# Stick-breaking attention: running sums from a rounded part and a rest, the two heads of a pair side by side

## The chip, the cores and the metric

One core of one Trainium2 chip. The metric is the device time of one execution in microseconds (us); lower is better.

## What is computed

The program is two layers of a hybrid block (feed-forward, a mixer of three branches, feed-forward) on 256 tokens of width 1024, and then a third block of another kind (delta rule, window attention, experts). The change is in one branch of the mixer, stick-breaking attention with 16 heads of 64:

```python
def _stick_breaking(qc, kc, vc):
    ...
    def block(args):
        qblk, qp = args
        z = jnp.einsum('bqhd,bkhd->bhqk', qblk, k).astype(jnp.float32) * scale
        strict = kpos[None, :] < qp[:, None]
        log_stay = jnp.where(strict, jax.nn.log_sigmoid(-z), 0.0)
        after = lax.cumsum(log_stay, axis=3, reverse=True) - log_stay
        a = jnp.where(strict, jnp.exp(jax.nn.log_sigmoid(z) + after), 0.0)
        return jnp.einsum('bhqk,bkhd->bqhd', a.astype(v.dtype), v)
```

The running sum over the keys is what the change is about. The kernel holds scores with the keys on the partitions, so that a running sum over keys is a product with a triangular matrix of ones.

## The kernel before

Most of the time goes to dense products whose weights stream in. A chunk of weights (128x1024 f32) is loaded by SyncE, ScalarE rounds it to fp32r (`hi`, L252), VectorE makes the rest (`lo`, L256), and TensorE adds three products, hi by hi, lo by hi and hi by lo (`three`, L281 to L283). The ring holds six chunks, so that rounding and splitting run up to six chunks ahead of the products.

Each engine has one queue, written out by hand. In the mixer (`Mixer.pe`, `.act`, `.dve`, L1719 on) the order follows a counter `h`, half a chunk of dense work on TensorE, and small steps of the branches are hung on values of `h`. Stick-breaking works on eight pairs of heads, one every five steps of `h` (`STICK = 5`; `pair_at(h, at)` gives the pair whose step `at` falls on `h`). A pair j has these steps, with the `h` of pair 0:

- TensorE, h = 5: `scores` (L1275, L1276), f32, into two banks, one for each head. The banks are shared by pairs of one parity.
- VectorE, h = 6: `dve_logits` scales and masks both heads (L1324) and takes the absolute value as max(-z, z) (L1327).
- ScalarE, h = 7: `act_log`, Exp (L1306) and Ln (L1308).
- VectorE, h = 9: `dve_stay` adds the positive part (L1332).
- TensorE, h = 10: `sums`, which waits for `stay`. For each head it is an f32 product with the triangle `from_` over 384 columns (L1284) and one with `ones` over 128 (L1285).
- VectorE, h = 11: `dve_shift` subtracts the sums from the logits (L1337).
- ScalarE, h = 12: `act_weights`, Exp (L1313).
- TensorE, h = 13: `outputs` (L1298 to L1300), f32.
- ScalarE, h = 14: `act_out` copies the 128x256 outputs out of PSUM (L1317). `scores` of pair j + 2 waits for it.

So `scores` of a pair and `sums` of the pair before it stand next to each other on TensorE. Near the end of the eight pairs the third branch starts: ScalarE makes a convolution's first tap at h = 42, 44 and 46 (L1361), VectorE the others from h = 44 to 52 (L1369, 4 instructions at each h), ScalarE applies Silu at h = 48, 51 and 54 (L1379). TensorE makes decays at h = 50 (L1461 to L1464), VectorE turns them into a table at h = 51 (`dve_cum`, its last instruction L1558), and TensorE turns the convolution's result at h = 54 (`turn_x`, L1470), which waits for that table.

GpSimd has a queue of its own. In the mixer it loads parameters, clears a pad and computes a power for another branch (L1105), and then waits for far later work. Elsewhere it multiplies rows for the third block (L910, L912) and splits a few chunks (L270).

## Time and profile before

| what | before |
|---|---|
| median of 3 runs | 2263.89 us (2263.28 to 2265.24) |
| the profiled execution, first to last instruction | 2268.0 us |
| that execution's own time, as far as recorded | its span, nothing around it is given |
| busy, TensorE matmul | 2207.9 us (97% of the span) |
| busy, VectorE | 1621.7 us (72%) |
| busy, ScalarE | 1161.0 us (51%) |
| busy, GpSimd | 364.9 us (16%) |
| mean granted TensorE clock | 0.980 |

The span is longer than the median of the runs without a profile by 4.1 us (0.2%). Busy shares are of one engine; a busy TensorE is one with a matmul in flight, and its instructions overlap by their pipelining, so that what a product costs is read from the distance of two starts. The steps of stick-breaking lie from about 372 to 472 us in the first layer and from about 1190 to 1290 us in the second.

### The profile page before, as it was taken

The numbers are of one execution on the slowest core, as the hardware profiler recorded it, in microseconds if no ns is written. First come the engines' busy times: TensorE is split into PE (matmuls) and PEld (weight loads), VectorE is DVE, ScalarE is ACT, GpSimd is POOL, SyncE is SP. The second block draws the span as 40 slices with busy tenths as digits, with TensorE's granted clock in tenths as the row PEclk, the third lists the DMA queues.
The fourth block names the chain that finished last, engine by engine and source line by source line (L and its number), as shares of the span: only waits on it lengthen the run. The fifth ranks groups of instructions, "written<-read, shape, count | busy, mean of one in ns | idle before, by whom it ended". The sixth has DMA issues, their size and how long they took to land.

```text
span 2268.0 us, 33371 instructions
## 1 busy us (share of the span) xinstructions
PE 2207.9 (97%) x12388; PEld 1862.2 (82%) x12388; DVE 1621.7 (72%) x2101; ACT 1161.0 (51%) x1720; POOL 364.9 (16%) x177
## 2 busy tenths in 40 slices
PE   7999999999999999999999999999988998999999
PEld 6888898878888888888988788788887987887777
DVE  5776676688767767766766798677687635658997
ACT  4445465575454444445555654444455515447875
POOL 1541000000025513511000000144202300000000
PEclk9999999999999999999999999999989877999999
DMA  9765644344667658756543345587542005559996
GB/s 307 232 229 165 206 146 135 118 149 140 203 213 238 227 170 262 231 185 204 158 141 122 120 158 186 169 262 237 185 145 76 3 6 164 188 189 320 360 360 220
DMA packets 320169, 426.92 MB, mean 188 GB/s; under 512 B 28192, under 2 KB 220080, under 8 KB 320032
## 3 DMA queue, kind: packets, MB, share of 16 engines
q1 hardware_dynamic: 315904, 412.45, 56.0%
q0 software_dynamic: 4016, 12.63, 2.1%
q8 instruction: 84, 1.38, 0.2%
q14 instruction: 53, 0.43, 0.1%
q10 hardware_dynamic: 112, 0.04, 0.0%
HBM read 423.97 MB, written 1.05 MB: 187 GB/s over the span
## 4 chain that ended last, share of the span: by engine, by line
PE 89%; DVE 6%; issue 1%; ACT 1%; DMA 1%; DVEq 1%; POOL 1%; SPq 0%; POOLq 0%; ACTq 0%
PE ps L281 20%; PE ps L283 20%; PE ps L282 20%; PE ps L644 10%; PE ps L3670 4%; DVE lo L256 1%; DVE room L1369 1%; PE ps L1284 1%; PE ps L630 1%; PE ps L331 1%; POOL lo L270 1%; PE ps L1126 1%; PE ps L2597 1%; PE ps L2581 1%; PE ps L2591 0%
## 5 line engine op out<-in xcount | busy, mean ns | idle before, releaser
L256 DVE TENSOR_TENSOR lo<-raw,hi 128x1024 fp32r<-128x1024 f32 (+1 forms) x727 | 1003.2, 1399 | 361.9 <-ACT hi L252 353.8
L252 ACT CAST hi<-raw 128x1024 fp32r<-128x1024 f32 (+1 forms) x737 | 766.2, 1048 | 581.2 <-PE ps L283 437.8
L281 PE MATMUL ps<-hi,xT_hi 128*128 128x512 f32 x1392 | 555.0, 399 | 5.9 <-issue 4.4
L283 PE MATMUL ps<-hi,xT_lo 128*128 128x512 f32 x1392 | 543.3, 390 | 0.0
L282 PE MATMUL ps<-lo,xT_hi 128*128 128x512 f32 x1392 | 542.5, 390 | 0.0
L281 PEld LDWEIGHTS ps<-hi,xT_hi 128*128 128x128 f32 x1392 | 262.8, 189 | 58.1 <-issue 6.0
L283 PEld LDWEIGHTS ps<-hi,xT_lo 128*128 128x128 f32 x1392 | 262.5, 189 | 56.0
L282 PEld LDWEIGHTS ps<-lo,xT_hi 128*128 128x128 f32 x1392 | 263.0, 189 | 50.4
L910 POOL TENSOR_SCALAR room<-room,vecs 128x1536 f32<-128x1536 f32 x28 | 133.3, 4762 | 233.7 <-DMA room<-in_w_ada 233.7
L281 PE MATMUL ps<-xT_hi,hi 128*128 128x256 f32 (+1 forms) x560 | 164.7, 294 | 0.9 <-DVE xT_lo L2350 0.9
L283 PE MATMUL ps<-xT_hi,lo 128*128 128x256 f32 (+1 forms) x560 | 159.4, 285 | 0.0
L282 PE MATMUL ps<-xT_lo,hi 128*128 128x256 f32 (+1 forms) x560 | 159.4, 285 | 0.0
L644 PE MATMUL ps<-hi,hidT_hi 128*128 128x512 f32 x352 | 137.6, 391 | 0.0
L644 PE MATMUL ps<-hi,hidT_lo 128*128 128x512 f32 x352 | 137.3, 390 | 0.0
L644 PE MATMUL ps<-lo,hidT_hi 128*128 128x512 f32 x352 | 137.0, 389 | 0.0
L281 PEld LDWEIGHTS ps<-xT_hi,hi 128*128 128x128 f32 (+1 forms) x560 | 106.9, 191 | 5.7 <-issue 5.0
L282 PEld LDWEIGHTS ps<-xT_lo,hi 128*128 128x128 f32 (+1 forms) x560 | 106.9, 191 | 0.4
L283 PEld LDWEIGHTS ps<-xT_hi,lo 128*128 128x128 f32 (+1 forms) x560 | 106.7, 190 | 0.3
L912 POOL TENSOR_TENSOR room<-room 128x1536 f32<-128x1536 f32 x28 | 103.0, 3679 | 8.1 <-issue 4.7
L281 PE MATMUL ps<-hi,brT_hi 128*128 128x512 f32 x224 | 90.5, 404 | 1.7 <-DVE brT_lo L341 1.7
L283 PE MATMUL ps<-hi,brT_lo 128*128 128x512 f32 x224 | 89.1, 398 | 0.0
L282 PE MATMUL ps<-lo,brT_hi 128*128 128x512 f32 x224 | 89.0, 397 | 0.0
(546 smaller groups left out, 3156.6 us busy)
## 6 DMA issues: line engine op xcount, KB each, us to landing
raw<-in_w_mix_in SPq DMA_DIRECT2D x368, 256.0 KB, 2.9
raw<-in_ffn_w_in SPq DMA_DIRECT2D x352, 256.0 KB, 3.3
raw<-in_ffn_w_out SPq DMA_DIRECT2D x176, 256.0 KB, 2.9
raw<-in_w_gate SPq DMA_DIRECT2D x128, 256.0 KB, 4.9
raw<-in_w_up SPq DMA_DIRECT2D x128, 256.0 KB, 6.6
raw<-in_w_down SPq DMA_DIRECT2D x128, 256.0 KB, 5.5
room<-in_w_ada SPq DMA_DIRECT2D x32, 768.0 KB, 6.4
raw<-in_w_branch SPq DMA_DIRECT2D x96, 256.0 KB, 2.9
```

The lines of the kernel that those rows point to most:

```text
L252: nc.scalar.copy(hi[c.hi_slot][:, 0:c.cols], raw[c.slot][:, 0:c.cols]).then_inc(rounded, 1)
L256: nc.vector.tensor_tensor(lo[c.slot][:, 0:c.cols], raw[c.slot][:, 0:c.cols], hi[c.hi_slot][:, 0:c.cols], ALU.subtract).then_inc(split, 1)
L270: nc.gpsimd.tensor_tensor(lo[c.slot][:, 0:c.cols], raw[c.slot][:, 0:c.cols], hi[c.hi_slot][:, 0:c.cols], ALU.subtract).then_inc(split, 1)
L281: pe.matmul(out, a[0], b[0], start=start, stop=False)
L282: pe.matmul(out, a[0], b[1], start=False, stop=False)
L283: return pe.matmul(out, a[1], b[0], start=False, stop=stop)
L331: ins = pe.transpose(ps[:, bank, at:at + P], self.src[:, t, k * P:(k + 1) * P], ident)
L630: ins = pe.transpose(ps[:, 6 + t, k * P:(k + 1) * P], hid[:, t, k * P:(k + 1) * P], ident)
L644: ins = pe.matmul(ps[:, 2 * t + half, :], a[p], w[q][:, cols], start=first and n == 0, stop=False, skip_group_check=True)
L910: nc.gpsimd.tensor_scalar(self.rows(k), self.rows(k), cols2[:, k:k + 1], None, ALU.mult)
L912: nc.gpsimd.tensor_tensor(pieces.acc, pieces.acc, self.rows(k), ALU.add).then_inc(pieces.multiplied, 1)
L3670: ins = pe.matmul(ps[:, self.sums(tile) + half, :], a[p], w[q][:, cols], start=first and n == 0, stop=False, skip_group_check=True)
```

## The change

The logarithms' sums (`stay`) are rounded to fp32r by ScalarE (`act_round`), the rest is made by GpSimd (`pool_rest`), and the sums are six fp32r products for a pair in place of four f32 ones. For that the two heads of a pair lie side by side, in three blocks of 2x128 columns: one block of 256 columns is the last key block, the other 512 fill a bank. `dve_logits` reorders them and takes two instructions for it. The outputs are copied by VectorE (`dve_out`) and no longer by ScalarE. The steps are moved: `sums` from h = 10 to 12, `dve_shift` from 11 to 13, `act_weights` from 12 to 14, `outputs` from 13 to 15, the copy of the outputs from 14 to 16; `act_round` is at h = 10. `scores` of pair j + 2 now waits for `shifted` of pair j, and `sums` for the copy of pair j - 2. Semaphores of two other classes are merged (`Scan`, `DeltaRule`) with the same waits as before; that part of the diff is left out but for one line.

```diff
         ("ident", p == j),
         ("ones", np.ones((P, P))),
+        ("from_", p >= j),
         ("upto", p <= j),
-        ("from_", p >= j),
...
-        z, lg = ([view(t, at + 768 * j, 2, 384) for t, at in ((scratch, 0), (room, R_GATES))] for j in range(2))
+        z = [view(scratch, 768 * j, 3, 2, P) for j in range(2)]
+        lg = [view(room, R_GATES + 768 * j, 3, 2, P) for j in range(2)]
+        lg_hi = [over(f"stick_hi{j}", [P, 768], "merged", 768 * j) for j in range(2)]
+        lg_lo = [over(f"stick_lo{j}", [P, 768], "room", R_GATES + 768 * j) for j in range(2)]
+        sum_ones = over("stick_ones", [P, 2 * P], "room", R_GATES + 1536)
...
         def scores(self, pe, j):
             g = j % 2
             if j > 1:
-                pe.wait_ge(self.copied, self.nth(j - 2))
+                pe.wait_ge(self.shifted, self.nth(j - 2))
...
         def sums(self, pe, j):
             g = j % 2
-            pe.wait_ge(self.stay, self.nth(j))
-            for e in range(2):
-                bank = ps[:, 2 * g + e, :]
-                pe.matmul(bank[:, 0:384], const("from_"), self.lg[g][:, e, :], start=True, stop=False)
-                ins = pe.matmul(bank[:, P:TOK], const("ones"), self.lg[g][:, e, TOK:384], start=False, stop=True)
-            ins.then_inc(self.summed, 1)
+            pe.wait_ge(self.rest, self.nth(j))
+            if j > 1:
+                pe.wait_ge(self.copied, self.nth(j - 2))
+            ones, from_ = self.sum_ones[:, 0:P], self.sum_ones[:, P:2 * P]
+            hi_, lo_ = self.lg_hi[g], self.lg_lo[g]
+            first, last = ps[:, 2 * g, :], ps[:, 2 * g + 1, 0:TOK]
+            pe.matmul(first, from_, hi_[:, 0:512], start=True, stop=False)
+            pe.matmul(first, from_, lo_[:, 0:512], start=False, stop=False)
+            pe.matmul(last, from_, hi_[:, 512:768], start=True, stop=False)
+            pe.matmul(last, from_, lo_[:, 512:768], start=False, stop=True)
+            pe.matmul(first[:, TOK:512], ones, hi_[:, 512:768], start=False, stop=False)
+            pe.matmul(first[:, TOK:512], ones, lo_[:, 512:768], start=False, stop=True).then_inc(self.summed, 1)
...
+        def act_ones(self, act):
+            act.wait_ge(consts_par, 16)
+            at = CONSTS["ones"][0]
+            nc.scalar.copy(self.sum_ones[:], consts[:, at:at + 2 * P])
+
+        def act_round(self, act, j):
+            g = j % 2
+            act.wait_ge(self.stay, self.nth(j))
+            nc.scalar.copy(self.lg_hi[g][:], self.lg[g].rearrange("p n e k -> p (n e k)")).then_inc(self.rounded, 1)
+
+        def pool_rest(self, eng, j):
+            g = j % 2
+            eng.wait_ge(self.rounded, self.nth(j))
+            nc.gpsimd.tensor_tensor(self.lg_lo[g][:], self.lg[g].rearrange("p n e k -> p (n e k)"), self.lg_hi[g][:], ALU.subtract).then_inc(self.rest, 1)
...
-        def act_out(self, act, j):
-            act.wait_ge(self.out_done, self.nth(j))
-            nc.scalar.copy(br[:, :, j * P:(j + 1) * P], self.out(j % 2)).then_inc(self.copied, 1)
+        def dve_out(self, dve, j):
+            dve.wait_ge(self.out_done, self.nth(j))
+            if j + 2 < self.PAIRS:
+                dve.wait_ge(self.scored, self.nth(j + 2))
+            nc.vector.tensor_copy(br[:, :, j * P:(j + 1) * P], self.out(j % 2)).then_inc(self.copied, 1)
 
         def dve_logits(self, dve, j):
...
-            V.scalar_tensor_tensor(out=self.z[g], in0=ps[:, 2 * g:2 * g + 2, 0:384], scalar=HDC ** -0.5,
-                                   in1=bc(const("stick_add").unsqueeze(1), [P, 2, 384]), op0=ALU.mult, op1=ALU.add)
+            mask = const("stick_add").rearrange("p (n k) -> p n k", n=3)
+            for e in range(2):
+                V.scalar_tensor_tensor(out=self.z[g][:, :, e, :], in0=ps[:, 2 * g + e, 0:384].rearrange("p (n k) -> p n k", n=3), scalar=HDC ** -0.5,
+                                       in1=mask, op0=ALU.mult, op1=ALU.add)
...
-        dt_abs, dt_log, decay_done = sem("b_dt_abs"), sem("b_dt_log"), sem("b_decay")
...
     # Mixer.pe
-                j = self.pair_at(h, 10)
+                j = self.pair_at(h, 12)
                 if j is not None:
                     stick.sums(pe, j)
-                j = self.pair_at(h, 13)
+                j = self.pair_at(h, 15)
                 if j is not None:
                     stick.outputs(pe, j)
...
     # Mixer.act
-                j = self.pair_at(h, 12)
+                if h == 8:
+                    stick.act_ones(act)
+                j = self.pair_at(h, 14)
                 if j is not None:
                     stick.act_weights(act, j)
                 j = self.pair_at(h, 7)
                 if j is not None:
                     stick.act_log(act, j)
-                j = self.pair_at(h, 14)
+                j = self.pair_at(h, 10)
                 if j is not None:
-                    if j == 0:
-                        act.wait_ge(feat_turned, self.turn_a.value(3))
-                    stick.act_out(act, j)
+                    stick.act_round(act, j)
...
     # Mixer.dve
-                j = self.pair_at(h, 11)
+                j = self.pair_at(h, 13)
                 if j is not None:
                     stick.dve_shift(dve, j)
+                j = self.pair_at(h, 16)
+                if j is not None:
+                    if j == 0:
+                        dve.wait_ge(feat_turned, self.turn_a.value(3))
+                    stick.dve_out(dve, j)
...
     # Layer.pool
             m.scan.load_norm(pool)
+            for j in range(StickBreaking.PAIRS):
+                m.stick.pool_rest(pool, j)
             pool.wait_ge(evac_dve, m.A.gate[1].evac_dve)
```

The lines of the changed kernel are other ones than those before: `scores` is L1279 and L1280 there, `sums` L1291 to L1296, `outputs` L1308 to L1310, the logarithm L1316 and L1318, the rounding L1328, the rest L1333, the weights' Exp L1338, the copy of outputs L1344, the logits L1353 and L1356, `stay` L1361, `shift` L1367, the taps L1391 and L1399, Silu L1409.

How the sums stand on TensorE. This is the difference on TensorE at h = 12 of the first layer, between two half chunks of dense work (L281 to L283):

```order
 L282 MATMUL ps<-xT_lo,hi_61 128x256
 L283 MATMUL ps<-xT_hi,lo_49 128x256
+L1291 MATMUL ps<-stick_hi_96,stick_ones 128x512 [waits c_rest]
+L1292 MATMUL ps<-stick_lo_98,stick_ones 128x512
+L1293 MATMUL ps<-stick_hi_96,stick_ones 128x256
+L1294 MATMUL ps<-stick_lo_98,stick_ones 128x256
+L1295 MATMUL ps<-stick_hi_96,stick_ones 128x256
+L1296 MATMUL ps<-stick_lo_98,stick_ones 128x256
 L281 MATMUL ps<-xT_hi,hi_61 128x256
 L282 MATMUL ps<-xT_lo,hi_61 128x256
```

The sums now stand alone between fp32r products; the outputs of pair j - 2 have moved to where they were, behind the scores of pair j.

The end of the eight pairs on VectorE, from h = 43 on, before:

```order
L256 TENSOR_TENSOR lo_57<-raw,hi_63 128x1024
L1332 SCALAR_TENSOR_TENSOR room<-room 128x768
L1369 SCALAR_TENSOR_TENSOR room<-room,vecs 128x256 x8
L256 TENSOR_TENSOR lo_58<-raw,hi_64 128x1024
L1337 TENSOR_TENSOR room<-room,ps 128x768
L1369 SCALAR_TENSOR_TENSOR room<-room,vecs 128x256 x8
```

and of the change, from the same chunk on:

```order
L256 TENSOR_TENSOR lo_57<-raw,hi_63 128x1024
L1361 SCALAR_TENSOR_TENSOR room<-ln_par,room 128x768
L1399 SCALAR_TENSOR_TENSOR room<-room,vecs 128x256 x8
L256 TENSOR_TENSOR lo_58<-raw,hi_64 128x1024
L1344 COPY hidden<-ps 128x2x128
L1399 SCALAR_TENSOR_TENSOR room<-room,vecs 128x256 x8
L256 TENSOR_TENSOR lo_59<-raw,hi_65 128x1024
L1367 TENSOR_TENSOR ln_par<-ln_par,ps 128x768
L1399 SCALAR_TENSOR_TENSOR room<-room,vecs 128x256 x8
```

The shift of pair 7 (L1337 before, L1367 now) has moved behind eight more taps, one more chunk and a copy of outputs.

The same end on ScalarE in the change, from h = 45 on:

```order
L1328 CAST stick_hi_97<-room 128x768
L252 CAST hi_64<-raw 128x1024
L1391 ACTIVATE room<-room,vecs 128x256 x4
L252 CAST hi_65<-raw 128x1024
L1409 ACT_TABLE_LOAD
L1409 ACTIVATE room<-room 128x1024
L1338 ACT_TABLE_LOAD
L1338 ACTIVATE ln_par<-ln_par 128x768
L1563 ACT_TABLE_LOAD
```

The weights of pair 7 (L1338) now come behind the first Silu, with a load of tables before them and one after.

## Rows read from the trace of the kernel before

**Rows 1.** The page, busy time of each engine.

```profile
PE 2207.9 (97%) x12388; PEld 1862.2 (82%) x12388; DVE 1621.7 (72%) x2101; ACT 1161.0 (51%) x1720; POOL 364.9 (16%) x177
```

**Rows 2.** Waits of TensorE, whole span: us in total, times, longest.

```profile
PE ps L1284 <- DVE room L1332: 4.1, 2, 2.1
PE ps L1284 <- DVE ln_par L1332: 2.9, 2, 1.4
...
PE ps L1470 <- DVE small L1558: 1.4, 2, 1.2
```

**Rows 3.** The chain of waits that ended last, 440 to 490 us: start, us, what.

```profile
450.88 0.64 PE ps L1275 x4
...
456.60 0.85 ACT room L1306
...
460.80 0.96 ACT hi L252
461.78 1.23 DVE lo L256
...
482.39 1.09 PE ps L1470 x8
```

**Rows 4.** Timeline of TensorE, scores and sums at h = 15: start, us.

```profile
394.69 0.28 PE L282 MATMUL ps<-xT_lo,hi 128*128 128x256 f32 x1
394.81 0.28 PE L283 MATMUL ps<-xT_hi,lo 128*128 128x256 f32 x1
395.02 0.71 PE L1275 MATMUL ps<-room 64*128 64x256 f32 x4
...
395.88 0.91 PE L1284 MATMUL ps<-room,consts 128*128 128x384 f32 x2
...
397.64 0.36 PE L281 MATMUL ps<-xT_hi,hi 128*128 128x256 f32 x1
397.84 0.28 PE L282 MATMUL ps<-xT_lo,hi 128*128 128x256 f32 x1
```

**Rows 5.** Timeline of TensorE, two neighbouring fp32r products of 512 columns.

```profile
480.15 0.39 PE L282 MATMUL ps<-lo,xT_hi 128*128 128x512 f32 x1
480.38 0.39 PE L283 MATMUL ps<-hi,xT_lo 128*128 128x512 f32 x1
```

**Rows 6.** Timeline of TensorE, outputs of pair 6 and what follows.

```profile
457.61 0.33 PE L1298 MATMUL ps<-room,ln_par 128*128 128x64 f32 x2
...
458.86 0.48 PE L281 MATMUL ps<-hi,xT_hi 128*128 128x512 f32 x1
```

**Rows 7.** Source L270: split of a chunk by GpSimd, ns min/median/max.

```profile
L270 POOL TENSOR_TENSOR lo<-raw,hi x10: 2397/2410/2417, 204.8 to 1464.4; 128x1024 fp32r<-128x1024 f32 x10
```

**Rows 8.** Groups of VectorE by form: busy us, mean ns of one.

```profile
L1235 DVE SCALAR_TENSOR_TENSOR ln_par<-room,ln_par 128x256 f32<-128x256 f32 x16 | 7.7, 479 | 0.0
L1324 DVE SCALAR_TENSOR_TENSOR room<-ps,consts 128x768 f32<-128x768 f32 x8 | 7.6, 950 | 0.0
L1211 DVE COPY room<-ps 128x256 f32<-128x256 f32 x16 | 6.7, 420 | 2.4 <-PE ps L1114 2.4
```

**Rows 9.** Timeline of VectorE and GpSimd, 59 to 67 us.

```profile
59.77 6.50 DVE L256 TENSOR_TENSOR lo<-raw,hi 128x1024 fp32r<-128x1024 f32 x3
...
59.41 3.51 POOL L912 TENSOR_TENSOR room<-room 128x1536 f32<-128x1536 f32 x1 [0.42 <-issue]
```

**Rows 10.** Timeline of VectorE, shift of pair 7 and the taps behind it.

```profile
468.61 0.95 DVE L1337 TENSOR_TENSOR room<-room,ps 128x768 f32<-128x768 f32 x1
469.48 3.25 DVE L1369 SCALAR_TENSOR_TENSOR room<-room,vecs 128x256 f32<-128x256 f32 x8
```

**Rows 11.** Timeline of ScalarE, a load of tables before the first Silu.

```profile
471.40 1.28 ACT L1379 ACT_TABLE_LOAD   x1
```

**Rows 12.** Windows, first layer, from sums 0 to sums 7: PE, PEld, DVE, ACT busy.

```profile
384.27:461.88 77.61, 77.50 (x501) 65.92 (x499) 48.11 (x57) 41.27 (x60) 0.00 (x0) 1.00 0.37 117
```

**Rows 13.** Windows, first layer, behind the wait of sums 7: granted clock is 0.50.

```profile
466.00:468.00 2.00, 2.00 (x7) 1.65 (x6) 1.93 (x5) 0.90 (x2) 0.00 (x0) 0.50 0.00 0
```

82 lines of the change are left out of this document (45 added, 37 removed).

## The prediction

> **What bounds the kernel now.** I read the busy shares first: TensorE has a matmul in flight for 97% of the span, VectorE works 72%, ScalarE 51%, GpSimd 16% [rows 1]. So a step costs what it takes on TensorE's queue, unless TensorE waits. Next the waits of TensorE: it waits for the logarithms (L1332) in front of the sums four times, 7.0 us in all, 1.4 us at pair 0 and 2.1 us at pair 7 in each layer, and twice for the decay table (L1558), 1.4 us in all [rows 2]. Then the chain of waits at the end of the eight pairs. It leaves TensorE behind the scores of pair 7 (start 450.88), goes over VectorE and ScalarE (Exp at 456.60, rounding of a chunk at 460.80), and from 461.78 on lies in VectorE's queue until TensorE's turn of the convolution at 482.39 [rows 3]. The reader should see two regimes in each layer: up to the scores of pair 7 the time is TensorE's, and from there to h = 54 it is VectorE's queue. What TensorE saves in the second stretch is worth nothing by itself.
>
> **TensorE, up to the scores of pair 7.** The f32 sums of a pair run from 395.88 to 397.64, 1.76 us [rows 4]. The new ones are two fp32r products of 512 columns and four of 256. Neighbours of these sizes start 0.23 us [rows 5] and 0.12 us [rows 4] apart, so 2 x 0.23 + 4 x 0.12 = 0.94 us, a saving of 0.82 us for a pair. Six pairs' sums (0 to 5) lie before this point: 4.9 us.
>
> Each group of f32 products also costs its borders. The scores start 0.21 us behind a product whose successor is due after 0.12, and behind the sums the second fp32r product comes 0.20 us after the first instead of 0.12 [rows 4]: 0.17 us for a group. Before, scores with the sums of the pair ahead were one group and outputs another, 14 up to here. Now the scores carry the outputs of pair j - 2 and the sums are fp32r, so that there are 8. Six fewer give 1.0 us. The outputs of pair 5, 1.25 us [rows 6], move behind this point; I count them below.
>
> The waits here: sums 0 waited 1.4 us. They now come two half chunks later. A half chunk is 12 products of 256 or 6 of 512 columns, 1.4 us either way, so 2.8 us, and a turn of eight transposes between them adds about 1. After the logarithms come a rounding, 3/4 of a chunk's 0.96 us [rows 3], and the rest on GpSimd, 3/4 of the 2.41 us of a chunk's split [rows 7], 1.8 us. GpSimd starts behind VectorE's next chunk, 1.2 us after the logarithms. The rest is there 1.4 + 1.2 + 1.8 + 0.1 = 4.5 us after TensorE's old arrival and TensorE 3.8 us after it: a wait of 0.7, a gain of 0.7.
>
> The middle pairs: from scores to sums TensorE now has seven half chunks (9.8), two groups of outputs (2.3), one of scores (0.9) and one of sums (0.9), 13.9 us. The chain behind the scores is: outputs of pair j - 2 (1.1), their copy (0.4), logits, the logarithm (two of 0.85 [rows 3]), a rounding of a chunk (1.0), its split (1.2), the shift of pair j - 1 (0.9), for even pairs the weights' Exp and another chunk on ScalarE (1.9; stay and the rounding lie beside it), that chunk's split, behind which GpSimd stands (1.2), and the rest (1.8). The logits in two instructions: 256 columns take 479 ns and 768 take 950 [rows 8], so 384 take about 0.60 and two 1.2, 0.25 us more than now. The copy is bounded by one of the same shape, 420 ns [rows 8]. With 2.2 for the logits, 1.7 for the logarithm and 0.4 for hand-overs the sum for an even pair is 13.8 us, a tie with 13.9; odd pairs have 2 us to spare. I charge 0.4 us for each of pairs 2, 4 and 6, 1.2 us; the bounds are 0 and a whole rest each, 5.4 us.
>
> Up to the scores of pair 7 a layer gains 4.9 + 1.0 + 1.25 + 0.7 - 1.2 = 6.65 us.
>
> **From there to h = 54.** The scores end 0.86 us [rows 4] after their start, at S = 451.7, and the turn starts at S + 30.7 [rows 3]. Before, the logits of pair 7 ended with the Exp's start at 456.6, S + 4.9, because the sums of pair 6 and their shift stood ahead of them. Now outputs 5, a copy, two halves and the absolute value do: 1.1 + 0.4 + 1.2 + 1.0 = 3.7. From there to VectorE's chunk at 461.78 it is 5.2 us of ScalarE as before, so S + 8.9 where it was S + 10.1. From that chunk to the turn it is 20.6 us [rows 3] of VectorE's queue. What joins it: the copies of pairs 6 and 7 (0.4 each) and what the rest of pair 7 on GpSimd takes from VectorE. No row shows GpSimd under the taps (L1369). The nearest is three chunks' splits from 59.77 on that take 6.50 us where three of 1.2 would take 3.6: they lose 2.9 us under a GpSimd product that ends at 62.92, 3.15 us after they began [rows 9]. So the cost lies between 0 and the 1.8 us of a rest; I take 1.8, as the taps too read two operands from SBUF. The Trainium skill, SBUF — State Buffer, section on the two separate sides, says that a VectorE instruction with two SBUF inputs and a GpSimd instruction that reads SBUF lock each other out for a whole instruction. By that rule the taps are held for the full rest and the term is as taken; if only some instructions were held, it would be smaller and the sum better by up to 3.6 us over the layers.
>
> S + 8.9 + 20.6 + 0.8 + 1.8 = S + 32.1, 1.4 us later than now. TensorE comes out at the same place. Its sums 7 wait some 1.5 us for the rest. The shift of pair 7 was 6.8 us behind that chunk's start (468.61 [rows 10]); eight more taps (3.25 [rows 10]), a chunk (1.2), a copy and the GpSimd's 1.8 stand ahead of it now, so it ends at S + 8.9 + 6.8 + 6.7 + 0.9, S + 23.3. With the Exp the outputs of pair 7 start at S + 24.2, where TensorE is ready at about S + 19.8: a new wait of over 4 us. Outputs, decays and four half chunks (7.8) end at S + 32.0. What stands behind that wait is all dense work, but VectorE's queue would hold it anyway.
>
> **What costs nothing.** Two more loads of tables in a layer, 1.28 us each [rows 11], fall on ScalarE while it would wait for the shift or has room before the next Silu, which itself waits for VectorE's taps; if that cover were gone, they cost 2.6 us a layer. The copy of the ones, once a layer, is under 0.4 us on ScalarE. The scores' new wait (for the shift of pair j - 2) ends earlier than their place. GpSimd has nothing behind the rests but parameter loads that waited until after h = 55. SyncE's queue is not touched. The reordered constants and merged semaphores move nothing.
>
> **The sum.** A layer gains 6.65 - 1.4 = 5.25 us, two layers 10.5. The profiled execution, 2268.0 us, would become 2257.5. The runs' median of 2263.89 is 4.1 us below it; the same difference there gives 2253.4 us. Behind h = 54 the queues stand to each other as before, so the gain stays.
>
> **Rivals.** (A) The waits go for good and VectorE's queue is not lengthened: the rest of pair 7 finds room, the even pairs' tie falls well. Then a layer gains eight savings (6.6), the borders (1.0) and the waits of 1.4 and 2.1 (3.5): 11.1, so 2241.7 us. For it speaks that VectorE is busy 48.1 of 77.6 us between sums 0 and 7 [rows 12]; against it the solid stretch from 461.78 on. Chance 0.13.
>
> (B) The move does nothing for the time. The even pairs wait 1.3 us each, and the long wait before outputs 7 costs clock too: after the wait of 2.1 us at sums 7 TensorE was granted 0.50, the lower level of 1.2 GHz, between 466 and 468 us [rows 13], which costs some 1.6 us. A layer gains 5.25 - 2.7 - 1.6 = 1, so 2262 us. Chance 0.15.
>
> (C) Slower. The rest is late for every pair, because GpSimd and VectorE hold each other: each rest takes its 1.8 us, the wait for a VectorE chunk ahead (1.2) and a start-up, and VectorE in turn loses 1.8 us to it, which moves the next logits. The chain of a pair then grows by 3 us; even pairs wait 3.4 and odd pairs 1. From 0.8 us of wait for every pair on, the gain is gone. With 2.2 on average, a layer loses 8 x 2.2 against the 6.65 + 1.2 gained before waits and the 1.4 behind S: 11 us a layer, 2286 us; with 1.6 it is 2277. Against it speaks that VectorE's chunks are rounded and split up to six ahead, so that it has slack between the steps. Chance 0.04.
>
> (D) The change doesn't do what it says, the fp32r products being no faster than f32 ones: 2268 with the later steps. Rows 4 and 5 exclude nearly all of it; it is in the 0.04.
>
> **How the numbers follow.** The forecast has 0.68, A 0.13, B 0.15, C with D 0.04. The forecast's own range takes in the bounds of its terms, 3.6 us better without the hold, and 5 worse with 0.9 us more wait for each even pair: 2249 to 2259. For 8 in 10 I go half way into A and to B: 2246 to 2261. A measurement can tell 0.2%, 4.5 us, so faster means below 2259.4: nearly all of the forecast, all of A and little of B, 0.83; the same 0.13; slower 0.04.
>
> **What would show it.** The sums (L1291 to L1296) should take 0.94 us a pair, and the windows up to the scores of pair 7 should be 6 to 7 us shorter in each layer. TensorE's list of waits should hold L1291 for the rest (L1333), under 1 us for even pairs and 1.5 us at pair 7, and one of about 4 us at the outputs of pair 7 (L1308). The rest should take 1.8 us, and taps beside it should show one stretched instruction. The turn of the convolution should come 32 us after the scores of pair 7. The prediction is wrong if waits at L1291 sum to over 10 us, if VectorE's queue from its chunk to the table takes no longer than 20.6 us, or if what is gained by h = 54 is lost behind it.

## The result and the profile after

The changed kernel is slower: 2275.74 us median (2271.85 to 2279.14, 6 runs) against 2264.56 us (2263.28 to 2267.59, 6 runs) before, ratio 1.004, interval 1.003 to 1.005: 0.4%, small but clear of noise. The forecast was 2253.4 us. In a second comparison (e12_change_again) it is 2274.38 against 2265.33, ratio 1.0039, 1.0025 to 1.0052. The profiled execution took 2276.91 us and its span is 2275.1 us, with a mean granted clock of 0.973 where it was 0.980.

The page of the changed kernel, busy time of each engine, answers to [rows 1]:

```profile
PE 2204.6 (97%) x12356; PEld 1863.0 (82%) x12356; DVE 1648.3 (72%) x2133; ACT 1172.2 (52%) x1726; POOL 397.3 (17%) x193
```

TensorE is hardly less busy, although 16 pairs' sums are 0.82 us shorter each. Either they are not shorter, or something else was lengthened. The timeline of TensorE, changed kernel, sums of pair 2 (start, us), answers to [rows 4]:

```profile
397.79 0.40 PE L1291 MATMUL ps<-stick_hi,stick_ones 128*128 128x512 f32 x1
398.02 0.40 PE L1292 MATMUL ps<-stick_lo,stick_ones 128*128 128x512 f32 x1
398.26 0.28 PE L1293 MATMUL ps<-stick_hi,stick_ones 128*128 128x256 f32 x1
398.38 0.28 PE L1294 MATMUL ps<-stick_lo,stick_ones 128*128 128x256 f32 x1
398.50 0.28 PE L1295 MATMUL ps<-stick_hi,stick_ones 128*128 128x256 f32 x1
398.61 0.28 PE L1296 MATMUL ps<-stick_lo,stick_ones 128*128 128x256 f32 x1
398.73 0.28 PE L281 MATMUL ps<-xT_hi,hi 128*128 128x256 f32 x1
```

From 397.79 to 398.73 it is 0.94 us, as worked out. The waits of TensorE over the whole span (us in total, times, longest) answer to [rows 2]:

```profile
PE ps L1308 <- ACT ln_par L1338: 7.7, 4, 4.0
PE ps L1279 <- DVE ln_par L1367: 5.9, 2, 2.9
...
PE ps L1291 <- POOL stick_lo L1333: 0.8, 2, 0.4
```

The waits in front of the sums are nearly gone (7.0 us before, 0.8 now). In their place stand two that the change made: the outputs (L1308) wait for the weights' Exp, and the scores of pair 7 (L1279) wait 2.9 us in each layer for a shift. The windows of the first layer around these two show the clock (the number after POOL's busy time):

```profile
444.00:448.00 4.00, 1.19 (x6) 0.65 (x4) 2.03 (x3) 1.87 (x3) 0.00 (x0) 1.00 0.44 131
448.00:452.00 4.00, 3.88 (x21) 3.63 (x22) 2.15 (x3) 3.46 (x4) 1.31 (x1) 0.58 0.02 6
452.00:456.00 4.00, 4.00 (x12) 3.14 (x12) 3.86 (x6) 1.45 (x2) 0.81 (x1) 0.56 0.05 4
...
472.00:476.00 4.00, 1.38 (x12) 1.38 (x13) 3.93 (x8) 2.58 (x4) 0.00 (x0) 1.00 0.06 22
476.00:480.00 4.00, 4.00 (x16) 3.04 (x16) 2.26 (x5) 4.00 (x4) 0.00 (x0) 0.50 0.00 0
480.00:484.00 4.00, 4.00 (x14) 3.11 (x13) 3.77 (x11) 2.88 (x4) 0.00 (x0) 0.65 0.43 131
```

Behind each wait TensorE is granted 0.50, its lower level of 1.2 GHz, for some 7 us, and does half as much. Added up over windows of 1 us, one such stretch cost 3.4 us of full clock (5.1, in 10 us, behind the outputs of pair 7 in the second layer). TensorE counts as fully busy in it, which is why its busy time did not fall.

The table puts the two layers side by side: starts of scores 0, of scores 7 and of the turn at h = 54; TensorE's waits in front of stick-breaking's steps and the turn; and the clock lost, which is the sum of one minus the granted clock over windows of 1 us.

| | scores 0 | scores 7 | turn | scores 0 to turn | waits | clock lost |
|---|---|---|---|---|---|---|
| before, layer 0 | 371.92 | 450.81 | 482.39 | 110.47 | 3.7 | 1.7 |
| before, layer 1 | 1190.39 | 1269.29 | 1300.88 | 110.49 | 5.1 | 0 |
| changed, layer 0 | 372.06 | 448.12 | 485.55 | 113.49 | 7.6 | 6.8 |
| changed, layer 1 | 1193.80 | 1269.86 | 1308.01 | 114.21 | 6.8 | 8.5 |

The change loses 3.0 and 3.7 us between scores 0 and the turn, nearly all of what the span grew (7.1 us); behind the turn both kernels take the same time (967.1 us from the second turn to the end, in both). The medians lie 11 us apart, 4 more than the two spans: the span before was 3.4 us above the median of its runs, the span after 0.6 us below its own.

### The profile page after: what moved, and what is told of

Its sections match the earlier page's. It is cut to its first block, busy times and chain, and to the rows that moved or that the text cites. A ratio compares the mean times of both kernels' runs of the same rounds, so it can differ in the third digit from the quotient of the medians.

```text
span 2275.1 us, 33383 instructions
## 1 busy us (share of the span) xinstructions
PE 2204.6 (97%) x12356; PEld 1863.0 (82%) x12356; DVE 1648.3 (72%) x2133; ACT 1172.2 (52%) x1726; POOL 397.3 (17%) x193
## 4 chain that ended last, share of the span: by engine, by line
PE 85%; DVE 7%; ACT 2%; issue 2%; DVEq 1%; DMA 1%; POOL 1%; SPq 0%; POOLq 0%; ACTq 0%
PE ps L281 20%; PE ps L283 19%; PE ps L282 19%; PE ps L644 10%; PE ps L3715 4%; DVE lo L256 2%; DVE room L1399 1%; ACT hi L252 1%; PE ps L630 1%; PE ps L331 1%; PE ps L1126 1%; DVE room L1356 1%; DVEq L1355 1%; PE ps L2642 1%; PE ps L2626 0%
## 5 line engine op out<-in xcount | busy, mean ns | idle before, releaser
L256 DVE TENSOR_TENSOR lo<-raw,hi 128x1024 fp32r<-128x1024 f32 (+1 forms) x727 | 1015.3, 1416 | 362.1 <-ACT hi L252 354.3
L281 PE MATMUL ps<-hi,xT_hi 128*128 128x512 f32 x1392 | 557.8, 401 | 5.9 <-issue 4.4
L283 PE MATMUL ps<-hi,xT_lo 128*128 128x512 f32 x1392 | 546.7, 393 | 0.0
L281 PEld LDWEIGHTS ps<-hi,xT_hi 128*128 128x128 f32 x1392 | 265.2, 190 | 59.0 <-issue 6.0
L283 PEld LDWEIGHTS ps<-hi,xT_lo 128*128 128x128 f32 x1392 | 264.5, 190 | 56.8
L281 PE MATMUL ps<-xT_hi,hi 128*128 128x256 f32 (+1 forms) x560 | 163.9, 293 | 0.9 <-DVE xT_lo L2394 0.9
L283 PE MATMUL ps<-xT_hi,lo 128*128 128x256 f32 (+1 forms) x560 | 158.7, 283 | 0.0
L281 PEld LDWEIGHTS ps<-xT_hi,hi 128*128 128x128 f32 (+1 forms) x560 | 106.1, 190 | 5.9 <-issue 5.0
L283 PEld LDWEIGHTS ps<-xT_hi,lo 128*128 128x128 f32 (+1 forms) x560 | 106.1, 189 | 0.3
L281 PE MATMUL ps<-hi,brT_hi 128*128 128x512 f32 x224 | 90.9, 406 | 1.7 <-DVE brT_lo L341 1.7
L283 PE MATMUL ps<-hi,brT_lo 128*128 128x512 f32 x224 | 89.6, 400 | 0.0
```

The lines of the kernel that those rows point to most:

```text
L256: nc.vector.tensor_tensor(lo[c.slot][:, 0:c.cols], raw[c.slot][:, 0:c.cols], hi[c.hi_slot][:, 0:c.cols], ALU.subtract).then_inc(split, 1)
L281: pe.matmul(out, a[0], b[0], start=start, stop=False)
L283: return pe.matmul(out, a[1], b[0], start=False, stop=stop)
```

## The experiments

Two theories of the wait at the scores of pair 7. **L**: it is a loop through the queues. The scores of pair j need the shift of pair j - 2. The chain of waits of the changed kernel, 439 to 449 us (start, us, what), shows it going from the logits of pair 6 over ScalarE into the chunk's split, behind which the shift of pair 5 stands:

```profile
441.25 0.93 DVE ln_par L1353 x2
442.18 0.07 issue
442.26 0.97 DVE room L1356
...
443.25 0.84 ACT room L1316
...
444.92 1.03 ACT hi L252
445.95 0.02 issue
445.97 1.22 DVE lo L256
447.20 0.88 DVE ln_par L1367
448.07 0.04 issue
448.12 0.73 PE ps L1279 x4
```

The shift needs none of this; the last product of its sums started at 440.81. It stands at h = 13 behind the split of the chunk, the chunk's cast stands on ScalarE behind the logarithm of the next pair, and that needs the next pair's logits, which stand on VectorE behind the steps of the pair before. So a pair cannot take less than this round through the two queues, and the logits of pairs 4 to 7 start 11.7 us apart on average (417.36 to 452.41) where TensorE would take 10.2 to 10.8. The two engines fall behind from pair to pair: the logits of pairs 4, 5 and 6 start 3.9, 5.3 and 6.7 us behind their scores, and at pair 7 TensorE has to wait.

**G**: GpSimd's rests hold VectorE. The timelines of VectorE and GpSimd, changed kernel, around two rests:

```profile
427.41 1.67 DVE L1576 TENSOR_TENSOR small<-room,vecs 128x32 f32<-128x32 f32 x1
...
437.21 0.19 DVE L1585 SCALAR_TENSOR_TENSOR small<-small,vecs 128x32 f32<-128x32 f32 x1
...
438.89 2.03 DVE L256 TENSOR_TENSOR lo<-raw,hi 128x1024 fp32r<-128x1024 f32 x1 [0.88 <-ACT hi L252]
...
426.88 2.16 POOL L1333 TENSOR_TENSOR stick_lo<-room,stick_hi 128x768 fp32r<-128x768 f32 x1 [10.86 <-ACT stick_hi L1328]
437.98 1.86 POOL L1333 TENSOR_TENSOR stick_lo<-room,stick_hi 128x768 fp32r<-128x768 f32 x1 [8.95 <-ACT stick_hi L1328]
```

An operation on 32 columns takes 1.67 us and ends with the rest (429.08, the rest at 429.04); its like outside a rest takes 0.19. A split takes 2.03 us instead of 1.23, and ends 1.08 us after the rest's end (439.84). The Trainium skill, SBUF — State Buffer, section on the two separate sides, says that the two engines lock each other out for a whole instruction when VectorE reads two operands from SBUF and GpSimd's instruction reads SBUF too; these rows agree.

In the tables below each experiment's ratio is to the kernel before in the same comparison, with its 95% interval.

### The two theories, one relief each

e1_no_rest: the rests are left out, and the products of the rest read the rounded part a second time, so the part of the logarithms that rounding loses is missing in the sums.

```diff
-            pe.wait_ge(self.rest, self.nth(j))
+            pe.wait_ge(self.rounded, self.nth(j))
...
-            hi_, lo_ = self.lg_hi[g], self.lg_lo[g]
+            hi_, lo_ = self.lg_hi[g], self.lg_hi[g]
...
-            for j in range(StickBreaking.PAIRS):
-                m.stick.pool_rest(pool, j)
```

> The changed kernel without GpSimd's rests: the products with the rest read the rounded part a second time and wait for the rounding, so TensorE does the same six products and the sums are less exact. Theory L (loop): VectorE and ScalarE pass each other work in a loop of about 11.6 us a pair against 10.4 us on TensorE, because a weight chunk's rounding stands behind the rounding of the logarithms on ScalarE and the shift stands behind that chunk's split on VectorE; GpSimd is only a small part: 2270 to 2274 us, the wait of TensorE at the scores of pair 7 still over 1 us. Theory G (GpSimd holds VectorE): each rest stretches one VectorE instruction by 0.6 to 1.5 us and that is what fills the loop: the wait at the scores is gone, the one at the outputs of pair 7 is under 2.5 us, 2256 to 2264 us.

e2_shift12: `dve_shift` at `pair_at(h, 12)` instead of 13, which puts it ahead of the split.

```diff
-                j = self.pair_at(h, 13)
+                j = self.pair_at(h, 12)
                 if j is not None:
                     stick.dve_shift(dve, j)
```

> The changed kernel with VectorE's shift one step earlier (h = 12 in place of 13), which puts it ahead of a weight chunk's split for every other pair. Theory L: the wait of 2.9 us at the scores of pair 7 goes in both layers, and with it the lower clock behind it (some 3 us a layer); the wait at the outputs of pair 7 gets shorter, as the shift then stands ahead of four taps and a chunk: 2262 to 2268 us. Theory G: the shift's place doesn't matter, as the queue is as full as before: 2273 to 2277 us.

e3_cast_first: `act_round` behind the chunk's cast at the end of the step.

```diff
-                j = self.pair_at(h, 10)
-                if j is not None:
-                    stick.act_round(act, j)
...
                 if h % 2 and h > 1:
                     tick_act(act, b.chunks[c])
+                j = self.pair_at(h, 10)
+                if j is not None:
+                    stick.act_round(act, j)
```

> The changed kernel with ScalarE's rounding of the logarithms behind the weight chunk's rounding of the same step, not ahead of it (odd pairs alone have both in one step). Theory L: the chunk no longer waits for stay, each odd pair takes about 1.5 us less in the loop, the wait at the scores of pair 7 goes: 2264 to 2270 us. Theory G: 2273 to 2277 us, since the rests hold VectorE as before.

e4_copy_act: the copies of the outputs on ScalarE again, still at h = 16. The logits of pair j + 2 now wait for the copy, as another engine makes it.

```diff
-                dve.wait_ge(self.out_done, self.nth(j - 2))
+                dve.wait_ge(self.copied, self.nth(j - 2))
...
+                    stick.act_out(act, j)
...
-                    stick.dve_out(dve, j)
```

> The changed kernel with the copy of the outputs on ScalarE again (at h = 16, the logits of pair j + 2 wait for it). It takes 0.4 us a pair off VectorE's queue and puts 0.4 us and a hand-over on ScalarE's. Theory L: a loop that goes over both engines gains nothing, as the logits now wait for ScalarE: 2273 to 2280 us. Theory G (VectorE is simply too full): 0.4 us a pair less on VectorE shortens the waits by 1 to 3 us a layer: 2269 to 2273 us.

| | median us | ratio | wait at scores 7 | scores 0 to turn, layers 0 and 1 |
|---|---|---|---|---|
| e1_no_rest | 2260.62 | 0.9979 (0.9970 to 0.9988) | none | 107.1, 107.1 |
| e2_shift12 | 2260.37 | 0.9981 (0.9971 to 0.9992) | none | 106.9, 107.1 |
| e3_cast_first | 2265.98 | 0.9999 (0.9990 to 1.0008) | 0.38 | 110.2, 108.8 |
| e4_copy_act | 2270.36 | 1.0017 (1.0008 to 1.0026) | 2.30 | 112.1, 109.5 |

Each theory was right about its own relief and wrong about the other's: L had named 2270 to 2274 us for e1_no_rest, G 2273 to 2277 for e2_shift12. So in this kernel each cause is needed for the wait and neither is enough. The round is set by the order, and it is too long by what the rests add to it; to relieve it at either place is enough. Moving one operation by a half chunk, with every rest in place, gives 2260.4 us, better than L had said (2262 to 2268, the half clock behind the wait included). The wait at the outputs of pair 7 fell with it, from 3.96 and 3.25 us to 2.6, and the clock lost behind it in the second layer from 5.1 to 3.4. In e1_no_rest that wait was 3.3 us, where G had named under 2.5. Of stick-breaking's steps in the second layer of e2_shift12, behind pair 0, these alone still waited (timeline of TensorE; the wait stands in brackets):

```profile
1268.10 0.43 PE L1308 MATMUL ps<-room,ln_par 128*128 128x64 f32 x2 [0.62 <-ACT ln_par L1338]
...
1272.96 0.50 PE L1291 MATMUL ps<-stick_hi,stick_ones 128*128 128x512 f32 x1 [0.49 <-POOL stick_lo L1333]
...
1280.89 0.43 PE L1308 MATMUL ps<-room,ln_par 128*128 128x64 f32 x2 [2.63 <-ACT ln_par L1338]
```

e3_cast_first is in L's range (2264 to 2270), though 0.38 us of the wait stayed. e4_copy_act moved 0.4 us a pair off VectorE and left most of the wait: the copy is a small part of the loop. It is in G's range (2269 to 2273) and below L's (2273 to 2280).

### The products alone, both reliefs, and the Exp

e5_f32_sums undoes the arithmetic and keeps the order; `act_ones`, `act_round` and `pool_rest` are left out with it.

```diff
-            pe.wait_ge(self.rest, self.nth(j))
+            pe.wait_ge(self.stay, self.nth(j))
...
+            lg = self.lg[g].rearrange("p n e k -> p (n e k)")
...
-            pe.matmul(first, from_, hi_[:, 0:512], start=True, stop=False)
-            pe.matmul(first, from_, lo_[:, 0:512], start=False, stop=False)
-            pe.matmul(last, from_, hi_[:, 512:768], start=True, stop=False)
-            pe.matmul(last, from_, lo_[:, 512:768], start=False, stop=True)
-            pe.matmul(first[:, TOK:512], ones, hi_[:, 512:768], start=False, stop=False)
-            pe.matmul(first[:, TOK:512], ones, lo_[:, 512:768], start=False, stop=True).then_inc(self.summed, 1)
+            pe.matmul(first, from_, lg[:, 0:512], start=True, stop=False)
+            pe.matmul(last, from_, lg[:, 512:768], start=True, stop=True)
+            pe.matmul(first[:, TOK:512], ones, lg[:, 512:768], start=False, stop=True).then_inc(self.summed, 1)
```

> The changed kernel with the sums in f32 again (three products instead of six, read from the logarithms themselves): no rounding, no rest, no copy of the ones; the layout, the later places of all steps and VectorE's copies stay. TensorE gets 0.82 us a pair more (6.6 a layer), VectorE is rid of GpSimd's hold and ScalarE of the rounding (0.83 us a pair). Theory G (GpSimd's hold makes the loop late): no wait at L1279, few waits before the sums, 2258 to 2266 us, below the changed kernel's 2275.7 although TensorE has more to do. Theory L (it is the place of the shift behind h = 13 in VectorE's queue that closes the loop): the wait at the scores of pair 7 stays at 1 us or more and the time is 2268 to 2276. If the moved steps alone were the whole loss, it would be above 2280.

e6_shift_cast is e2_shift12 with e3_cast_first.

> The changed kernel with both reliefs of the loop: the shift at h = 12 and the rounding behind the chunk's cast on ScalarE. Each alone took the wait at the scores of pair 7 away. Theory L: the second has little left to relieve, 2258 to 2262, as with the shift alone (2260.4). If what is left of the loss is the late logarithm of pair 7 and not the loop, the later rounding makes the wait at the sums longer (1.4 us or more at pair 7) and it is 2261 to 2266.

e7_shift_weights is e2_shift12 with `act_weights` at `pair_at(h, 13)` instead of 14.

> The changed kernel with the shift at h = 12 and the weights' Exp at h = 13, so that the Exp of pair 7 stands ahead of the first Silu (h = 48) in ScalarE's queue and no table is loaded back and forth there. Theory K (the wait of 2.6 us at the outputs of pair 7 costs itself and then half the clock for about 3 us in each layer): the wait falls under 1.2 us, no half clock behind it, 2254 to 2258. Theory V (VectorE's queue holds the turn of the convolution anyway): the wait shrinks, a wait appears at the turn or the decays instead, 2259 to 2262.

e8_rest_vector is e7_shift_weights with the rest on VectorE at h = 11.

```diff
-            nc.gpsimd.tensor_tensor(self.lg_lo[g][:], ...
+            nc.vector.tensor_tensor(self.lg_lo[g][:], ...
...
+                j = self.pair_at(h, 11)
+                if j is not None:
+                    stick.pool_rest(dve, j)
```

> As e7_shift_weights, but the rest of the logarithms is made by VectorE at h = 11 (about 1 us a pair) and not by GpSimd. Theory G (under a rest of GpSimd VectorE loses about as much as the rest would take it itself, some 7 us a layer): within 3 us of e7_shift_weights, no VectorE instruction stretched in the eight pairs. If the hold were cheap (under 0.3 us a pair), VectorE would be 5 to 6 us a layer more busy and the time 4 us or more above e7_shift_weights.

| | median us | ratio | scores 0 to scores 7 | scores 0 to turn |
|---|---|---|---|---|
| e5_f32_sums | 2267.53 | 1.0011 (1.0002 to 1.0020) | 75.8 | 110.3, 109.0 |
| e6_shift_cast | 2260.30 | 0.9979 (0.9970 to 0.9988) | 72.4 | 107.2, 107.1 |
| e7_shift_weights | 2265.88 | 1.0001 (0.9992 to 1.0010) | 73.1 | 108.8, 108.5 |
| e8_rest_vector | 2264.76 | 1.0003 (0.9994 to 1.0013) | 74.0 | 109.3, 108.4 |

With f32 sums in the same order there is no wait at the scores of pair 7, and the kernel is faster than the changed one by 8 us with more work on TensorE. So the new places alone do not lose what the change lost (2.5 us of the 11 stay). That the wait went fits the rests and the rounding being gone from the round, but TensorE is also slower here (its scores 4 to 7 start 11.0 to 11.4 us apart), which leaves the round more time; this run does not part the two. It came out 1.5 us above the range that G named and 0.5 below L's, whose wait of 1 us or more is absent; a wait of 2.6 us at the outputs of pair 7 and 3.4 and 1.7 us of clock lost behind it are there too.

e6_shift_cast shows that the second relief adds nothing to the first. The wait at the sums of pair 7 grew to 1.42 us, and the one at its outputs shrank from 2.64 to 1.85. e7_shift_weights was a miss for both of its theories. To save two loads of tables the Exp of every pair was moved a half chunk ahead, into a place where ScalarE stands and waits for the shift with the casts behind it: the wait at the sums of pair 7 grew from 0.48 to 1.74 us, and the turn waited for VectorE by 2.7 us in layer 1.

e8_rest_vector weighs the hold. The windows of the first layer from 372.9 to 452.7 us (TensorE, weight load, VectorE, ScalarE, GpSimd), e7_shift_weights:

```profile
372.90:452.70 79.80, 77.73 (x532) 68.46 (x531) 64.22 (x90) 45.30 (x61) 13.85 (x8) 1.00 0.42 131
```

and e8_rest_vector:

```profile
372.90:452.70 79.80, 77.30 (x531) 68.47 (x530) 64.32 (x96) 45.18 (x61) 0.60 (x1) 1.00 0.41 129
```

Its rests among VectorE's groups (busy us, mean ns of one):

```profile
L1333 DVE TENSOR_TENSOR stick_lo<-room,stick_hi 128x768 fp32r<-128x768 f32 x16 | 15.2, 952 | 0.0
```

VectorE is busy 64.2 us with the rests on GpSimd, and 64.3 with the rests its own, each 0.95 us. The two windows do not hold quite the same instructions. e10_pair7_cum and e14_no_rest_pair7, which come below, differ in the rests alone and do, 129 in each from scores 0 to the turn:

```profile
371.97:473.91 101.94, 99.14 (x649) 86.33 (x648) 85.48 (x129) 63.67 (x85) 15.81 (x9) 1.00 0.43 132
371.20:471.18 99.98, 98.79 (x650) 86.33 (x649) 79.32 (x129) 63.69 (x85) 0.60 (x1) 1.00 0.42 133
```

So eight rests on GpSimd stretch VectorE's instructions by 6.2 us, 0.77 us each. Making a rest on GpSimd took four fifths or more of the VectorE time that making it there takes. The time of e8_rest_vector, 1.1 us below e7_shift_weights, is within the 3 us that G had named; with it came a wait of 4.4 us at the sums of pair 7, for VectorE's rest.

### The tail of pair 7, and the clock

In e2_shift12 the outputs of pair 7 still waited 2.6 us, and 7 us at half clock followed. Three versions ask what that wait is worth.

e9_pair7_early:

```diff
-                j = self.pair_at(h, 13)
+                j = 7 if h == 46 else self.pair_at(h, 12) if h != 47 else None
                 if j is not None:
                     stick.dve_shift(dve, j)
...
-                j = self.pair_at(h, 14)
+                j = 7 if h == 47 else self.pair_at(h, 14) if h != 49 else None
                 if j is not None:
                     stick.act_weights(act, j)
```

> The changed kernel with the shift at h = 12 for pairs 0 to 6 and, for pair 7 alone, the shift at h = 46 on VectorE (ahead of a copy and two groups of taps) and the weights' Exp at h = 47 on ScalarE (ahead of the first Silu). With the shift at h = 12 alone the shift of pair 7 stood at 462.37 us though its sums were complete at 459.0, and its Exp started at 464.86 behind the first Silu and a table load. Theory K (a wait of 2.6 us at the outputs of pair 7 costs itself and half the clock for 7 us behind it): the outputs of pair 7 wait under 0.5 us, the granted clock stays at 1.00 up to the turn, and a layer gains 3 us or more: 2252 to 2256 us. Theory V (VectorE's queue, busy but for 0.4 us from the stay of pair 7 to the turn, holds the turn anyway): the wait comes back at the turn or the decays, a layer gains 0 to 1.3 us: 2258 to 2261.

e10_pair7_cum adds to it:

```diff
-                if h == 51:
+                if h == 50:
                     scan.dve_cum(dve, 1)
```

> As e9_pair7_early, and the copies of the decay sums (the four small operations that the turn waits for) at h = 50 on VectorE, ahead of a chunk's split, an addition and a copy. Theory V: the turn no longer waits for VectorE's queue, 2 us a layer below e9_pair7_early if that had a wait at the turn, 2254 to 2257. Theory K: no difference from e9_pair7_early (within 1.5 us), since there was no wait at the turn.

e11_outputs_later is e2_shift12 with:

```diff
-                j = self.pair_at(h, 15)
+                j = 7 if h == 52 else self.pair_at(h, 15) if h != 50 else None
                 if j is not None:
                     stick.outputs(pe, j)
...
-                j = self.pair_at(h, 16)
+                j = 7 if h == 53 else self.pair_at(h, 16) if h != 51 else None
```

> The changed kernel with the shift at h = 12, and the outputs of pair 7 at h = 52 instead of h = 50 on TensorE (their copy at h = 53): two more half chunks (2.7 us) ahead of them, the length of the wait that they had (2.64 us). Nothing is taken from VectorE or ScalarE. Theory K (the wait and the half clock behind it): no wait of over 0.5 us, clock 1.00 up to the turn; TensorE is 4 us a layer earlier at the turn unless VectorE holds it: 2252 to 2257 us. Theory V: the turn waits instead, 2259 to 2262. If the half clock is set by something other than the idle time of TensorE, it appears here too.

e12_change_again is the changed kernel itself.

> The changed kernel as it is, once more, beside the three others on the same chip. All theories: 2272 to 2279 us, ratio to before 1.003 to 1.005, with waits of 2.9 us at the scores of pair 7 and 3.2 to 4.0 at its outputs in both layers, each followed by the granted clock 0.50 for 6 to 8 us.

| | median us | ratio | outputs 7 wait | turn waits | clock lost up to the turn | scores 0 to turn |
|---|---|---|---|---|---|---|
| e9_pair7_early | 2260.76 | 0.9980 (0.9971 to 0.9989) | none | 4.1 | 0 | 105.3, 105.3 |
| e10_pair7_cum | 2257.12 | 0.9964 (0.9951 to 0.9978) | none | 0.7 | 0 | 101.9, 101.9 |
| e11_outputs_later | 2262.98 | 0.9990 (0.9981 to 0.9999) | none | 4.2 | 0, 0.4 | 105.4, 105.4 |
| e12_change_again | 2274.38 | 1.0039 (1.0025 to 1.0052) | 4.0 | none | 6.8, 6.8 | 113.8, 114.0 |

Each of the two theories was half right. The wait at the outputs went, and the clock stayed at 1.00 up to the turn (K); but the time came back as a wait at the turn, for the copies of the decay sums in VectorE's queue, and e9_pair7_early is no faster than e2_shift12 (V). Waits of TensorE, e9_pair7_early:

```profile
PE ps L1507 <- DVE small L1595: 8.1, 2, 4.1
...
PE ps L1291 <- POOL stick_lo L1333: 1.8, 4, 0.5
```

In e11_outputs_later the half clock appeared at the wait at the turn instead (3.4 us lost in each layer, in layer 1 from within the wait on), so that it follows TensorE's idle time wherever that is; it was slower than either theory had said. e10_pair7_cum fell 0.1 us above what V named (2254 to 2257), 3.6 us below e9_pair7_early and so 2.1 below what K allowed. In its trace four small operations (L1591 to L1595) no longer stand behind four taps, two additions for a gate (L1055) and a copy, and it has the clock at 1.00 throughout (windows of e10_pair7_cum, first layer):

```profile
468.00:476.00 8.00, 7.26 (x36) 5.81 (x35) 7.69 (x19) 5.97 (x5) 0.00 (x0) 1.00 0.44 133
476.00:484.00 8.00, 5.85 (x29) 4.35 (x28) 6.73 (x13) 5.58 (x6) 0.00 (x0) 1.00 0.43 130
```

e10_pair7_cum beats both kernels: 0.36% below the one before, 17 us below the changed one. Not all of the turn's gain is kept: from the second turn to the end of the span it takes 970.2 us where the two kernels take 967.1, since behind the turn VectorE and ScalarE come last (a second turn waits 0.9 us in each layer for VectorE's copy; the overlaps, L1515, wait 1.3 us in each layer for ScalarE's copies).

### What the products are worth in the right order

e13_f32_pair7 is e10_pair7_cum with the edit of e5_f32_sums; e14_no_rest_pair7 is e10_pair7_cum with that of e1_no_rest, so the same part of the sums is missing.

> As e10_pair7_cum (the places of the steps as there), but with the sums in f32 again, no rounding, no rest, no copy of the ones: what the rounded products are worth once the order is right. Theory T (TensorE's time up to the scores of pair 7 counts in full, as 0.82 us a pair): 6.5 us a layer above e10_pair7_cum's 2257.1, less what TensorE waited there, 2266 to 2271. Theory H (GpSimd's hold on VectorE and the rounding give back most of it, VectorE's queue ends the stretch): 2257 to 2263.

> As e10_pair7_cum, without GpSimd's rests: the second product of each pair reads the rounded part again, so the part of the logarithms lost in rounding is left out of the sums. TensorE's work is the same. It measures GpSimd's hold with the order right. Theory H: VectorE's queue gets 1.4 us shorter from the stay of pair 7 to the turn, the turn's waits of 0.7 and 0.9 us go, 2253 to 2256. If the hold costs nothing where no wait hangs on it: 2257, as e10_pair7_cum.

| | median us | ratio | scores 0 to scores 7 | scores 0 to turn |
|---|---|---|---|---|
| e13_f32_pair7 | 2262.05 | 0.9985 (0.9976 to 0.9994) | 75.8 | 104.4, 104.4 |
| e10_pair7_cum | 2257.12 | 0.9964 (0.9951 to 0.9978) | 72.4 | 101.9, 101.9 |
| e14_no_rest_pair7 | 2252.90 | 0.9945 (0.9931 to 0.9958) | 72.0 | 100.0, 100.0 |

The products are worth 4.9 us for both layers by the medians of two comparisons. Their intervals overlap at the edge, but the traces bear it out, 2.5 us a layer from scores 0 to the turn. TensorE's saving in this order is 16 x 0.80 = 12.8 us (the scores of pairs 5 and 6 start 10.99 us apart with the f32 sums and 10.19 with the new ones). The rests take 4.2 of the rest (e14_no_rest_pair7 against e10_pair7_cum; 3.9 by the traces). That is the hold on VectorE together with TensorE's own waits for the rests, 0.41 and 0.49 us a layer, and no run parts the two. The other 3.7 us are given up to VectorE's and ScalarE's queues near the turn, which does not depend on TensorE alone; how they divide was not tried. Theory H named 2257 to 2263 and 2253 to 2256 and missed the second by 0.1, while T named 2266 to 2271 for e13_f32_pair7, so H is the better one. Steps moved rightly, with the old products in the new layout, give 3.5 us.

## Why the prediction was wrong

**What bounds the kernel, TensorE and then VectorE's queue.** Right for the kernel before. In the changed one TensorE was the late one at the turn, too; e9 and e10, without the half clock, show VectorE's queue as the bound there again.

**The sums, 0.82 us a pair.** Right on TensorE, to the hundredth (0.94 us from the first product to the one behind the last).

**Borders of f32 groups, 1.0 us a layer.** Wrong. The scores of pairs 5 and 6 start 11.00 us apart before and 10.19 in e2_shift12, 0.81 us less; with a border of 0.17 saved for each pair it would be 0.99. The timelines of TensorE show why. The group that went, the outputs of a pair by themselves, had no border ahead of it (it started 0.23 us behind a dense product, as dense products do) and 0.09 us behind it; and behind the scores the outputs take 1.36 us in place of 1.25.

**The wait at sums 0, a gain of 0.7 us.** Right and small: it fell from 1.4 to 0.41 us, a gain of 1.0. But a wait of 0.53 us at a turn behind it (L331, for VectorE's L341), which the kernel before does not have, takes half of that back in each layer.

**"The scores' new wait (for the shift of pair j - 2) ends earlier than their place."** This is the step that failed, and it was costed at nothing with no row or chain behind it. The chain I drew ran from scores to sums, and charged 1.2 us a layer there; the shift of pair j - 1 was in it as a load of 0.9 us. I did not ask what stands ahead of the shift on VectorE. That is a chunk's split, which waits for a cast, which waits for the logarithm of the next pair. Measured: 2.93 and 2.92 us at the scores of pair 7. The delay grows with the pairs, since VectorE's logits come 11.7 us apart and TensorE's scores 10.2 to 10.8: the outputs of pair 4, behind the scores of pair 6, waited 0.27 us, the scores of pair 7 the 2.93. At the sums, where I looked for it, only pair 0 waited.

**"What stands behind that wait is all dense work, but VectorE's queue would hold it anyway."** The second failure. The wait at the outputs of pair 7 was foreseen at over 4 us and was 3.96 and 3.25. The clock behind it was seen in [rows 13] and waved off. It cost 3.4 us in layer 0 and 5.1 in layer 1, and the wait at the scores of pair 7 cost another 3.4 in each, so that TensorE was the late one at the turn, and not VectorE. The step before it, that VectorE's queue holds the turn until S + 32.1, was sound: in e9_pair7_early, where nothing else does, the turn comes at S + 32.0.

**S + 32.1 for the turn.** Measured 485.55 - 448.12 - 0.86, S + 36.6, 4.5 us later. TensorE was ready for the outputs of pair 7 at S + 21.7, which is the S + 19.8 of the prediction, 3.4 later for the half clock and 1.5 earlier, as the wait at the sums of pair 7 did not come. The outputs started at S + 25.6 and not S + 24.2, and from there to the turn it took 10.9 us and not 7.8, with 3.4 of clock lost. From e10_pair7_cum to the changed kernel the waits up to the turn grew by 5.3 and 4.6 us and the clock lost by 6.8 and 8.5, together 12.1 and 13.1; the turn came 11.6 and 12.3 us later, so these two account for all of it.

**The sum.** Minus 5.25 us a layer was forecast, plus 3.0 and 3.7 came, 8.3 and 9.0 apart. Of this, 3.8 lie ahead of the scores of pair 7, where 6.65 was to be gained and 2.8 was: the scores' wait (2.9), the outputs' wait of 0.27 ahead of them, the borders (1.0) and the wait at L331 (0.5), with the 1.2 charged for even pairs, which did not come, and the 0.3 more at sums 0 on the other side; some 0.5 us is left open. The other 4.5 and 5.2 lie between there and the turn: the half clock and the later outputs of pair 7.

**The loads of tables at no cost.** Not contradicted, not cleanly tested: e7_shift_weights took them away and lost by what it moved with them, and e9_pair7_early has none of them ahead of the outputs but moved the shift as well.

**GpSimd's hold.** Taken at 1.8 us once in a layer, for the taps. It was 1.4 us there (eight taps 4.86 us from 461.87 on where 3.41 is usual), but it falls on all eight pairs, and it was left out of the chain of the middle ones: 0.77 us a pair by e10_pair7_cum against e14_no_rest_pair7. The rest itself, 1.8 us, was right: 1.81 at the least.

**Behind h = 54 the gain stays.** Right, for what came in its place: both kernels take 967.1 us from the second turn to the end.

**The rivals.** C had half of the cause, GpSimd and VectorE holding each other so that the next logits come late; it lacked the place of the shift, and the clock. Its 2277 us is 1 us off, but by luck: it expected the wait at every pair's sums, 1.6 us each, and got 0.05. B had both waits and clock and valued the clock at 1.6 us a layer, a fourth to a fifth of the 6.8 and 8.5 that it cost here; its even pairs' waits did not come. The trace of before held the material for both: had the scores' wait been followed back over VectorE's and ScalarE's queues, slower would have deserved more than its 0.04.

## What to carry to other kernels

When a change puts a new wait in front of an engine that was never late, follow it back through the queue of the engine that serves it: what stands ahead of the awaited instruction there counts, and what that one waits for, until you come back to where you began. If you do, it is a loop, and its length is the least time of a turn. A wait of some 3 us on TensorE cost up to twice its length here, for the clock behind it; and an operation of this kind given to GpSimd, while VectorE works on two operands from SBUF, has to be charged to VectorE as well. When a new wait is found, move the awaited instruction before changing the arithmetic: here one half chunk was worth some 14 us.

## What the chip showed that was not expected

- Idle time of TensorE and the granted clock. In the stretch of stick-breaking, every wait of 2.5 to 4.4 us went with 0.50, mostly right behind it: for some 7 us, a loss of 3.4 us (once 5.1, in 10 us), or for half as long, a loss of 1.7. The shorter loss came at the outputs of pair 7 in the second layers of e3_cast_first (3.20 us of wait), e4_copy_act (2.85) and e5_f32_sums (2.55), at the turn in e9_pair7_early (4.1, both layers) and in the second layer of e7_shift_weights (2.7), and at the sums of pair 7 in the second layer of e8_rest_vector (4.4). The wait of 2.30 us at the scores of pair 7 in e4_copy_act cost 3.4 in layer 0 and nothing in layer 1, the wait of 2.05 us in the kernel before 1.7 in layer 0 and nothing in layer 1. In e7_shift_weights two waits of 1.74 and 1.67 us, 7 us apart, were followed by a loss of 3.4 in layer 0 and none in layer 1; in e6_shift_cast 1.42 and 1.85, 7 us apart, by 3.4 in both. Behind a wait of 1.25 us at the outputs of pair 6 e3_cast_first lost 1.7 in layer 0 and nothing in layer 1, and e4_copy_act lost 1.7 in layer 1. The kernel before lost nothing behind 1.43 us at sums 0; behind waits of 1.0 us and less alone no run lost any. What decides between the two layers stays open.
- GpSimd's subtract on 768 columns, 1.81 us alone, holds the VectorE instruction with two operands from SBUF that starts under it: one that takes 0.19 us ended with the rest, a split 1.08 us behind its end. And it takes 2.16 us itself when one is under way as it begins (the split of 426.10 was until 427.33, the rest began at 426.88).
- The 0.17 us at a border between f32 and fp32r products did not add up: six groups fewer in a layer were not faster by them.
